# A hybrid decoder trunk with top-2 experts: order of the h links among the weight splits, and 64-row writes of the light experts' results

## Chip, cores and metric

The kernel runs on one core of one Trainium2 chip. The metric is the device time of one execution in microseconds (us). Two DeepNorm layers are computed for 256 tokens of width 1024; the second layer has eight experts.

## The reference, cut to what matters

```python
D_MODEL, SEQ, N_EXPERTS, TOP_K, D_FF_EXPERT = 1024, 256, 8, 2, 3584

def swiglu(x, wg, wu, wd):
    return (jax.nn.silu(x @ wg) * (x @ wu)) @ wd

def moe_swiglu(x, w_router, we_gate, we_up, we_down):
    logits = (x @ w_router).astype(jnp.float32)
    top_vals, top_idx = lax.top_k(logits, TOP_K)
    gates = jax.nn.softmax(top_vals, axis=-1)
    combine = jnp.einsum("bske,bsk->bse", jax.nn.one_hot(top_idx, N_EXPERTS), gates)
    out = jnp.zeros_like(x)
    for e in range(N_EXPERTS):
        out = out + combine[..., e:e + 1] * swiglu(x, we_gate[e], we_up[e], we_down[e])
    return out

for i in range(2):
    mix = hybrid_mixer(x, ...)                         # short convolution and spatial gating
    x = layer_norm(ALPHA * x + mix, ln1_g[i], ln1_b[i])
    ffn = swiglu(...) if i == 0 else moe_swiglu(...)   # layer 1: the experts
    x = layer_norm(ALPHA * x + ffn, ln2_g[i], ln2_b[i])
```

All tensors are float32. The change touches only the expert layer, which fills the span from about 380 us on.

## The kernel before, in words

**Pieces of weights.** All weights come from DRAM in pieces of 1 MB (128 partitions x 2048 float32), by DMAs that SyncE issues (`load`, L405) into a ring of six slots, `raw`. Each float32 product is made from rounded parts: ScalarE rounds a piece into `w_hi` (`split_hi`, L615, its copy is L620), VectorE subtracts it from the whole into `w_lo` (`split_lo`, L981, its subtraction is in the helper at L979), and TensorE multiplies with both. `w_hi` and `w_lo` have four slots each. So `split_hi(p)` waits for the landing of piece p and for TensorE's last use of piece p-4, `split_lo(p)` waits for `split_hi(p)`, and SyncE issues piece p+6 when `split_lo(p)` is done.

**Steps.** Each expert's inner width is cut into 7 steps of 512 columns, which makes 56 steps. A step takes six pieces: two of gate, two of up, two of down. With b = `step_at(i)`, pieces b and b+1 are the gate of step i, b+2 and b+3 its up, b+4 and b+5 the down of step i-1, and b+6 begins the gate of step i+1. The four experts with the most tokens are "heavy" (H, up to 128 tokens, three matmuls for each weight block), the four others "light" (L, up to 64 tokens, whose two rounded parts stand side by side, two matmuls for each block). `ORDER` (L75) fixes the order: four H, then L and H by turns with three extra H, then seven L.

**The engines' order in step i**, written out by hand. TensorE (L2173): gate of i; the turning of h of step i-1 (`turn_h`: four transposes, L1965, for H; sixteen folding matmuls, L1972, for L), which signals `e_hT`; the up of i; the down of i-1 (L1631 to L1633 for H, L2009 and L2010 for L), which waits for the low part of h (`e_hT_lo`) and for the two down pieces.

ScalarE (L872): where i-1 is light, the copy of its up sums (L809); split_hi of b+1 to b+4; `leave_gate(i)` (L803 or L805, reads the gate sums); then the links of h: for H `round_h(i-1)` (L813) after `e_hT`, for L `silu_few(i-1)` (L817) after `e_hT` and `round_few(i-1)` (L821) after VectorE's `times_few`; then split_hi of b+5 and b+6. VectorE (L1489): split_lo of b+1 to b+4; for H `rest_of_h` (L1354), for L `times_few` (L1358) and `rest_of_few` (L1362), all after ScalarE's links; split_lo of b+5 and b+6; where i is heavy, `times_up(i)` (L1350).

Both engines work in order: an instruction that waits holds all that stand behind it.

**Results.** When an expert is complete, ScalarE copies its sums to `ys_rows` (L841; for a light one 64 rows at L839, to which VectorE adds the other half of the sums, L1376) and GpSimd writes them to `slot_rows` in DRAM (L572), all 128 rows whatever the expert. Seven experts are written so: four heavy, three light (the last light one stays on the chip). After the last write GpSimd gathers for each token the rows of its two experts from `slot_rows` (L597), by row numbers that VectorE works out in `usable_choices` (L1406) in step 2, with 128 rows for each expert; VectorE adds them in steps 53 and 54 (L1466).

Of the kernel before, what the change touches and what calls it, by code (L numbers as in the profile page):

```python
# [4 lines left out]
P = 128  # L5
# [9 lines left out]
def hybrid_trunk_kernel(nc, x_in, w_in, conv_w, v_g, v_b, w_s, b_s, out_g, w_out, ln1_g, ln1_b, ln2_g, ln2_b,  # L15
# [62 lines left out]
    def light(i):  # L78
        return ORDER[i] == "L"
# [13 lines left out]
    def block_of(kind, k):  # L93
        return k if kind == "H" else HEAVIES + k
# [28 lines left out]
    with ctx:  # L123
# [56 lines left out]
        slot_rows = nc.dram_tensor("slot_rows", [(E - 1) * P, D], f32, kind="Internal").ap()  # L180
# [81 lines left out]
        combine_last = ranking[:, 304:304 + NT]  # L262
        usable_rows, usable_gates, usable_tmp = (ranking[:, a:a + NT * E].rearrange("p (n e) -> p n e", n=NT)
# [246 lines left out]
        def _(pool):  # L510
# [57 lines left out]
            def write_rows(j):  # L568
                kind, k = KEPT[j]
                r0 = block_of(kind, k) * P  # L570
                pool.wait_ge(ys_kept, j + 1)
                pool.dma_start(slot_rows[r0:r0 + P, :], ys_rows[:]).then_inc(ys_written, 16)  # L572
# [32 lines left out]
        def _(act):  # L605
# [16 lines left out]
            def splits(first, last):  # L622
                for p in range(first, last + 1):
                    split_hi(p)
# [247 lines left out]
            for i in range(N_STEPS):  # L872
                b = step_at(i)
                if i:
                    if light(i - 1):
                        leave_up(i - 1)
                    splits(b + 1, b + 2)
                    if kept_at(i) is not None:
                        keep_ys(kept_at(i))
                    splits(b + 3, b + 4)  # L880
                leave_gate(i)
                if i == 0:
                    split_hi(b + 4)
                elif light(i - 1):
                    silu_few(i - 1)
                    round_few(i - 1)
                    splits(b + 5, b + 6)
                else:
                    round_h(i - 1)
                    splits(b + 5, b + 6)  # L890
                after_up(i)
# [76 lines left out]
        def _(dve):  # L968
# [410 lines left out]
            def over_tokens(a):  # L1379
                return a.unsqueeze(1).to_broadcast([P, NT, E])  # L1380
# [25 lines left out]
            def usable_choices():  # L1406

                for a, first in ((is_light, 0.0), (block_at, 0.0), (not_last, 1.0)):
# [3 lines left out]
                step(nc.vector.tensor_scalar_add(block_at[:, 1:E], ranks, 1.0 - LIGHTS))  # L1412
# [4 lines left out]
                step(nc.vector.scalar_tensor_tensor(out=block_at, in0=is_light, scalar=float(HEAVIES + LIGHTS - 1),  # L1417
                                                    in1=block_at, op0=ALU.mult, op1=ALU.add))
                step(nc.vector.scalar_tensor_tensor(out=wide_count, in0=slot_iota[:, 0:E], scalar=-1.0 / 16,
# [5 lines left out]
                step(nc.vector.scalar_tensor_tensor(out=usable_rows, in0=over_tokens(block_at), scalar=float(P),  # L1425
# [63 lines left out]
            for i in range(N_STEPS):  # L1489
                b = step_at(i)  # L1490
                if i:
                    splits(b + 1 if i > 1 else b + 2, b + 3)
                    if kept_at(i) is not None and KEPT[kept_at(i)][0] == "L":
                        fold_ys(kept_at(i))
                    split_lo(b + 4)
                if i == 0:
                    splits(b + 4, b + 5)
                elif light(i - 1):
                    times_few(i - 1)
                    rest_of_few(i - 1)  # L1500
                    splits(b + 5, b + 6)
                else:
                    rest_of_h(i - 1)
                    splits(b + 5, b + 6)
                if not light(i):
                    times_up(i)
                after_up(i)
# [737 lines left out]
```

## Time and profile before

| | us |
|---|---|
| median of 3 runs (1306.07 to 1307.63) | 1307.62 |
| the profiled execution, its own time | 1306.71 |
| its span, first to last instruction | 1305.0 |
| TensorE busy | 1242.2 (95%) |
| VectorE busy | 1105.3 (85%) |
| ScalarE busy | 930.3 (71%) |
| GpSimd busy | 49.5 (4%) |

The span is 1.7 us shorter than the execution's own time, and that is 0.9 us below the median. The mean granted TensorE clock is 0.994 of full speed. The DMA engines moved 435 MB; in the 40 equal slices of the span their mean busy share is nine tenths or more from the thirteenth slice to the thirty-ninth. A busy share is an average: which engine sets the time of a stretch is read from the waits and the timeline. Where a matmul row shows 0.39 us, the next one starts 0.23 us later, since matmuls are pipelined.

### The profile page before, as it was taken

To read this page: it belongs to the slowest core of one execution; us is meant where nothing else is said; L and a number is where in the kernel's file an instruction comes from. 1 tells how busy PE (TensorE), PEld (TensorE's weight loads), DVE (VectorE), ACT (ScalarE), POOL (GpSimd) and SP (SyncE) were. 2 spreads that over 40 slices of the span, in tenths; PEclk is the share of its full clock that TensorE was granted. 3 is DMA by queue.
4 is the path that set the end of the run, shared out by engine and by line. 5 is a ranking of instruction groups with operands and counts; after the bars stand their busy time and mean duration, and the time that the engine had idled before them with its cause. 6 is when DMAs were issued, how large, how long until landed. Compare 5 with 4: busy or idle time off the path is not lost.

```text
span 1305.0 us, 15584 instructions
## 1 busy us (share of the span) xinstructions
PE 1242.2 (95%) x6145; PEld 1026.3 (79%) x6145; DVE 1105.3 (85%) x872; ACT 930.3 (71%) x747; POOL 49.5 (4%) x57
## 2 busy tenths in 40 slices
PE   9999999999999999999999999999999999998875
PEld 8988888888887877878777777777788777777654
DVE  6987555577989999989898989988989998898886
ACT  5575444464877887877777878777778877786773
POOL 0100000001012000000000000000000000000010
PEclk9999999999999999999999999999999999999999
DMA  9948555546569999999999999999999999999991
GB/s 321 344 143 272 187 189 191 193 140 215 190 221 347 398 397 390 398 399 398 397 389 400 397 401 397 397 389 397 396 395 400 397 396 398 397 396 403 397 397 69
DMA packets 190082, 435.25 MB, mean 334 GB/s; under 512 B 8196, under 2 KB 50228, under 8 KB 175668
## 3 DMA queue, kind: packets, MB, share of 16 engines
q1 hardware_dynamic: 186272, 421.06, 86.7%
q0 software_dynamic: 3648, 13.11, 3.0%
q8 instruction: 50, 0.82, 0.3%
q14 instruction: 28, 0.23, 0.0%
q10 hardware_dynamic: 84, 0.02, 0.0%
HBM read 428.40 MB, written 5.77 MB: 333 GB/s over the span
## 4 chain that ended last, share of the span: by engine, by line
PE 41%; DVE 32%; DMA 18%; ACT 7%; issue 2%; SPq 0%; DVEq 0%; ACTq 0%
DVE w_lo L979 28%; DMA raw<-in_we_down 17%; ACT w_hi L620 7%; PE turn L1743 4%; PE turn L1740 4%; PE accp L1631 4%; PE accp L1632 4%; PE accp L1633 4%; PE turn L1631 3%; PE turn L1633 3%; PE turn L1632 3%; PE turn L1742 2%; PE turn L1741 2%; DVE y_work L1350 1%; PE turn L1972 1%
## 5 line engine op out<-in xcount | busy, mean ns | idle before, releaser
L979 DVE TENSOR_TENSOR w_lo<-raw,w_hi 128x2048 fp32r<-128x2048 f32 (+1 forms) x401 | 895.6, 2266 | 112.9 <-ACT w_hi L620 110.9
L620 ACT CAST w_hi<-raw 128x2048 fp32r<-128x2048 f32 x395 | 749.7, 1912 | 161.6 <-DMA raw<-in_we_up 59.5
L1998 PE MATMUL turn<-w_hi,t_both 128*128 128x512 f32 x448 | 185.2, 413 | 16.2 <-DVE w_lo L979 13.1
L1999 PE MATMUL turn<-w_lo,t_both 128*128 128x512 f32 x448 | 177.4, 396 | 0.0
L1631 PE MATMUL turn<-w_hi,a_hi 128*128 128x512 f32 x440 | 174.3, 396 | 1.8 <-DVE w_lo L979 1.2
L1633 PE MATMUL turn<-w_hi,a_lo 128*128 128x512 f32 x440 | 171.6, 390 | 0.0
L1632 PE MATMUL turn<-w_lo,a_hi 128*128 128x512 f32 x440 | 171.4, 390 | 0.0
L1998 PEld LDWEIGHTS turn<-w_hi,t_both 128*128 128x128 f32 x448 | 85.3, 191 | 53.7 <-DVE w_lo L979 34.5
L1631 PE MATMUL accp<-w_hi,hT_hi 128*128 128x512 f32 x224 | 90.5, 404 | 16.3 <-DVE hT_lo L979 16.3
L1631 PEld LDWEIGHTS turn<-w_hi,a_hi 128*128 128x128 f32 x440 | 82.7, 188 | 19.5 <-DVE w_lo L979 1.8
L1999 PEld LDWEIGHTS turn<-w_lo,t_both 128*128 128x128 f32 x448 | 85.4, 191 | 15.9
L1633 PEld LDWEIGHTS turn<-w_hi,a_lo 128*128 128x128 f32 x440 | 82.6, 188 | 17.6
L1632 PEld LDWEIGHTS turn<-w_lo,a_hi 128*128 128x128 f32 x440 | 82.7, 188 | 16.3
L2009 PE MATMUL accp<-w_hi,hT_hi 128*128 128x512 f32 x216 | 85.8, 397 | 10.2 <-DVE w_lo L979 7.9
L1740 PE MATMUL turn<-t_both,w_hi 128*128 128x512 f32 x232 | 91.8, 396 | 0.0
L1743 PE MATMUL turn<-t_both,w_hi 128*128 128x512 f32 x232 | 91.8, 396 | 0.0
L1632 PE MATMUL accp<-w_lo,hT_hi 128*128 128x512 f32 x224 | 88.1, 393 | 0.0
L1633 PE MATMUL accp<-w_hi,hT_lo 128*128 128x512 f32 x224 | 87.8, 392 | 0.0
L2010 PE MATMUL accp<-w_lo,hT_hi 128*128 128x512 f32 x216 | 84.3, 390 | 0.0
L1631 PEld LDWEIGHTS accp<-w_hi,hT_hi 128*128 128x128 f32 x224 | 42.3, 189 | 33.9 <-DVE hT_lo L979 25.6
L1742 PE MATMUL turn<-t_both,w_lo 128*128 128x256 f32 x232 | 64.6, 278 | 0.0
L1741 PE MATMUL turn<-t_both,w_lo 128*128 128x256 f32 x232 | 64.3, 277 | 0.0
(291 smaller groups left out, 1591.7 us busy)
## 6 DMA issues: line engine op xcount, KB each, us to landing
raw<-in_we_gate SPq DMA_DIRECT2D x112, 1024.0 KB, 10.2
raw<-in_we_up SPq DMA_DIRECT2D x112, 1024.0 KB, 11.3
raw<-in_we_down SPq DMA_DIRECT2D x112, 1024.0 KB, 10.6
raw<-in_w_in SPq DMA_DIRECT2D x18, 1024.0 KB, 9.0
raw<-in_w_down SPq DMA_DIRECT2D x11, 1024.0 KB, 5.0
raw<-in_w_gate SPq DMA_DIRECT2D x10, 1024.0 KB, 5.2
raw<-in_w_up SPq DMA_DIRECT2D x10, 1024.0 KB, 5.2
raw<-in_w_out SPq DMA_DIRECT2D x8, 1024.0 KB, 10.3
```

Of the source, the lines that this page charges most:

```text
L620: nc.scalar.copy(w_hi[:, p % PARTS, :], raw[:, p % RING, :]).then_inc(hi_done, 1)
L979: return nc.vector.tensor_tensor(out, whole, hi.bitcast(f32), ALU.subtract)
L1631: nc.tensor.matmul(to, lh, rh, start=start, stop=False, **group)
L1632: nc.tensor.matmul(to, lh, rl, start=False, stop=False, **group)
L1633: return nc.tensor.matmul(to, ll, rh, start=False, stop=stop, **group)
L1740: nc.tensor.matmul(whole, wh[:, k, at], xT_pair[:, k, :], start=(k == 0), stop=False)
L1741: nc.tensor.matmul(first, wl[:, k, at], xT_hi[:, k, :], start=False, stop=False)
L1742: nc.tensor.matmul(first, wl[:, k + 1, at], xT_hi[:, k + 1, :], start=False, stop=False)
L1743: last = nc.tensor.matmul(whole, wh[:, k + 1, at], xT_pair[:, k + 1, :], start=False, stop=(k == KD - 2))
L1998: nc.tensor.matmul(to, few[:, k, :], wh[:, kk, :], start=(k == 0), stop=False)
L1999: last = nc.tensor.matmul(to, few[:, k, :], wl[:, kk, :], start=False, stop=(k == KD - 1))
L2009: nc.tensor.matmul(accp[:, 2 + c, :], left, wh[:, j, cols], start=(first and j == 0), stop=False)
```

## The change

The rows of the light results lie in `slot_rows` behind those of the heavy ones, 64 for each (`first_row` takes the place of `block_of`); GpSimd writes 64 rows for a light expert; `usable_choices` works out the first row in units of 64, with two more small instructions. On ScalarE in each step from 1 on, the first link of h stands behind split_hi of b+3, that is ahead of split_hi of b+4 and of `leave_gate(i)`; a light h's second link, `round_few`, stands behind split_hi of b+4. `leave_gate(i)` follows. On VectorE the first link (`times_few`, or `rest_of_h` for a heavy h) stands ahead of split_lo of b+4 and a light h's `rest_of_few` behind it. The order of TensorE and of SyncE is not changed, and neither are the ring of six slots and the four slots of `w_hi` and `w_lo`.

```diff
--- before.py
+++ after.py
@@ -90,8 +90,8 @@
     def rank(kind, k):
         return k if kind == "L" else LIGHTS + k - 1
 
-    def block_of(kind, k):
-        return k if kind == "H" else HEAVIES + k
+    def first_row(kind, k):
+        return k * P if kind == "H" else HEAVIES * P + k * FEW
 
     LAST_ONE = ("L", LIGHTS - 1)
     FETCHED = (("L", 0), ("H", 1), ("L", 1), ("H", 2), ("L", 2), ("H", 3), LAST_ONE)
@@ -177,7 +177,7 @@
         ys_rows = sb("ys_rows", [P, D])
         more_rows = sb("more_rows", [P, D])
 
-        slot_rows = nc.dram_tensor("slot_rows", [(E - 1) * P, D], f32, kind="Internal").ap()
+        slot_rows = nc.dram_tensor("slot_rows", [HEAVIES * P + (LIGHTS - 1) * FEW, D], f32, kind="Internal").ap()
         token_rows = nc.dram_tensor("token_rows", [TOK, D], f32, kind="Internal").ap()
 
         v = work[:, 0:1024].rearrange("p (n c) -> p n c", n=NT)
@@ -260,6 +260,7 @@
         wide_slot = ranking[:, 280:280 + NT * E].rearrange("p (n e) -> p n e", n=NT)
         wide_count = ranking[:, 296:296 + E]
         combine_last = ranking[:, 304:304 + NT]
+        light_less = ranking[:, 306:306 + E]
         usable_rows, usable_gates, usable_tmp = (ranking[:, a:a + NT * E].rearrange("p (n e) -> p n e", n=NT)
                                                  for a in (320, 336, 352))
 
@@ -567,9 +568,10 @@
 
             def write_rows(j):
                 kind, k = KEPT[j]
-                r0 = block_of(kind, k) * P
+                r0 = first_row(kind, k)
                 pool.wait_ge(ys_kept, j + 1)
-                pool.dma_start(slot_rows[r0:r0 + P, :], ys_rows[:]).then_inc(ys_written, 16)
+                count = FEW if kind == "L" else P
+                pool.dma_start(slot_rows[r0:r0 + count, :], ys_rows[0:count, :]).then_inc(ys_written, 16)
 
             def fetch_tokens(f):
                 pool.wait_ge(tokens_known, f // 2 + 1)
@@ -877,17 +879,19 @@
                     splits(b + 1, b + 2)
                     if kept_at(i) is not None:
                         keep_ys(kept_at(i))
-                    splits(b + 3, b + 4)
+                    split_hi(b + 3)
+                    if light(i - 1):
+                        silu_few(i - 1)
+                        split_hi(b + 4)
+                        round_few(i - 1)
+                    else:
+                        round_h(i - 1)
+                        split_hi(b + 4)
                 leave_gate(i)
-                if i == 0:
-                    split_hi(b + 4)
-                elif light(i - 1):
-                    silu_few(i - 1)
-                    round_few(i - 1)
+                if i:
                     splits(b + 5, b + 6)
                 else:
-                    round_h(i - 1)
-                    splits(b + 5, b + 6)
+                    split_hi(b + 4)
                 after_up(i)
             leave_up(N_STEPS - 1)
             split_hi(MOE_AT + MOE_PIECES - 1)
@@ -1409,20 +1413,25 @@
                     nc.vector.memset(a[:, 0:1], first)
                 nc.vector.tensor_scalar(is_light[:, 1:E], ranks, LIGHTS - 0.5, None, ALU.is_lt)
                 nc.vector.tensor_scalar(not_last[:, 1:E], ranks, float(rank(*LAST_ONE)), None, ALU.not_equal)
-                step(nc.vector.tensor_scalar_add(block_at[:, 1:E], ranks, 1.0 - LIGHTS))
+                step(nc.vector.tensor_scalar(block_at[:, 1:E], ranks, float(P // FEW), (1.0 - LIGHTS) * (P // FEW),
+                                             ALU.mult, ALU.add))
+                step(nc.vector.scalar_tensor_tensor(out=light_less, in0=is_light, scalar=FEW / P - 1.0, in1=block_at,
+                                                    op0=ALU.mult, op1=ALU.mult))
                 nc.vector.scalar_tensor_tensor(out=wide_slot, in0=over_tokens(is_light), scalar=float(FEW),
                                                in1=slot_of[:, :, 0:E], op0=ALU.mult, op1=ALU.add)
                 nc.vector.scalar_tensor_tensor(out=wide_count, in0=is_light, scalar=float(FEW), in1=key,
                                                op0=ALU.mult, op1=ALU.add)
-                step(nc.vector.scalar_tensor_tensor(out=block_at, in0=is_light, scalar=float(HEAVIES + LIGHTS - 1),
+                step(nc.vector.scalar_tensor_tensor(out=block_at, in0=is_light,
+                                                    scalar=float(HEAVIES * P // FEW + LIGHTS - 1),
                                                     in1=block_at, op0=ALU.mult, op1=ALU.add))
+                step(nc.vector.tensor_tensor(block_at, block_at, light_less, ALU.add))
                 step(nc.vector.scalar_tensor_tensor(out=wide_count, in0=slot_iota[:, 0:E], scalar=-1.0 / 16,
                                                     in1=wide_count, op0=ALU.mult, op1=ALU.add))
                 step(nc.vector.tensor_reduce(most, wide_count, X, ALU.max))
                 nc.vector.tensor_copy(most_i, most[0:1, :])
                 nc.vector.scalar_tensor_tensor(out=usable_tmp, in0=wide_slot, scalar=P - 0.5, in1=over_tokens(not_last),
                                                op0=ALU.is_lt, op1=ALU.mult)
-                step(nc.vector.scalar_tensor_tensor(out=usable_rows, in0=over_tokens(block_at), scalar=float(P),
+                step(nc.vector.scalar_tensor_tensor(out=usable_rows, in0=over_tokens(block_at), scalar=float(FEW),
                                                     in1=slot_of[:, :, 0:E], op0=ALU.mult, op1=ALU.add))
                 nc.vector.tensor_tensor(usable_rows, usable_rows, usable_tmp, ALU.mult)
                 nc.vector.tensor_tensor(usable_gates, combine, usable_tmp, ALU.mult)
@@ -1492,16 +1501,16 @@
                     splits(b + 1 if i > 1 else b + 2, b + 3)
                     if kept_at(i) is not None and KEPT[kept_at(i)][0] == "L":
                         fold_ys(kept_at(i))
-                    split_lo(b + 4)
                 if i == 0:
                     splits(b + 4, b + 5)
                 elif light(i - 1):
                     times_few(i - 1)
+                    split_lo(b + 4)
                     rest_of_few(i - 1)
                     splits(b + 5, b + 6)
                 else:
                     rest_of_h(i - 1)
-                    splits(b + 5, b + 6)
+                    splits(b + 4, b + 6)
                 if not light(i):
                     times_up(i)
                 after_up(i)
```

## Rows read from the trace of the kernel before

**Rows 1.** Busy time by stretches: the engines, granted clock, DMA share, GB/s.

```profile
core 0: us, PE busy (x) PEld busy (x) DVE busy (x) ACT busy (x) POOL busy (x), PEclk, DMA share, GB/s
457.84:1183.14 725.30, 698.25 (x3221) 564.41 (x3220) 658.10 (x381) 576.25 (x419) 10.52 (x12) 1.00 1.04 397
1183.14:1272.01 88.87, 72.86 (x321) 55.23 (x320) 75.64 (x45) 66.25 (x52) 5.72 (x4) 0.96 1.04 398
```

**Rows 2.** Waits between 560 and 1250 us: total us, times, longest.

```profile
DVE w_lo L979 <- ACT w_hi L620: 60.1, 97, 2.8
...
ACT w_hi L620 <- DMA raw<-in_we_up: 52.9, 67, 3.4
...
ACT w_hi L620 <- DMA raw<-in_we_down: 23.3, 42, 0.7
```

**Rows 3.** Timeline of ScalarE: start, us, engine, line, operation, idle before.

```profile
1055.26 1.91 ACT L620 CAST w_hi<-raw 128x2048 fp32r<-128x2048 f32 x1 [0.56 <-DMA raw<-in_we_down]
...
1058.16 0.39 ACT L817 ACTIVATE few_work<-turn 128x256 f32<-128x256 f32 x1 [0.51 <-PE turn L1972]
1059.86 0.41 ACT L821 CAST hT_hi<-few_work 128x256 fp32r<-128x256 f32 x1 [1.31 <-DVE few_work L1358]
1060.17 5.53 ACT L620 CAST w_hi<-raw 128x2048 fp32r<-128x2048 f32 x3
...
1071.06 1.91 ACT L620 CAST w_hi<-raw 128x2048 fp32r<-128x2048 f32 x1 [0.52 <-DMA raw<-in_we_down]
...
1073.35 0.59 ACT L813 CAST hT_hi<-turn 128x512 fp32r<-128x512 f32 x1
1073.83 1.92 ACT L620 CAST w_hi<-raw 128x2048 fp32r<-128x2048 f32 x1
```

**Rows 4.** Timeline of VectorE in the same stretch.

```profile
1062.11 4.50 DVE L979 TENSOR_TENSOR w_lo<-raw,w_hi 128x2048 fp32r<-128x2048 f32 x2 [1.39 <-ACT w_hi L620]
1066.52 0.68 DVE L1350 TENSOR_TENSOR y_work<-turn,y_work 128x512 f32<-128x512 f32 x1
1067.12 8.89 DVE L979 TENSOR_TENSOR w_lo<-raw,w_hi 128x2048 fp32r<-128x2048 f32 x4
```

**Rows 5.** Timeline of TensorE in the same stretch, at the joints of its work.

```profile
1056.14 1.98 PE L1972 MATMUL turn<-fold,y_work 128*128 128x64 f32 x16
...
1067.12 0.39 PE L1998 MATMUL turn<-w_hi,t_both 128*128 128x512 f32 x1
...
1069.46 0.50 PE L1998 MATMUL turn<-w_hi,t_both 128*128 128x512 f32 x1 [0.37 <-DVE w_lo L979]
...
1071.42 0.63 PE L1965 MATMUL turn<-ident,y_work 128*128 128x128 f32 x4
...
1076.67 0.50 PE L1631 MATMUL accp<-w_hi,hT_hi 128*128 128x512 f32 x1 [0.67 <-DVE hT_lo L979]
...
1082.24 0.39 PE L1631 MATMUL turn<-w_hi,a_hi 128*128 128x512 f32 x1
...
1087.69 1.98 PE L1972 MATMUL turn<-fold,y_work 128*128 128x64 f32 x16
```

**Rows 6.** Timeline of VectorE near the end.

```profile
1260.80 4.49 DVE L979 TENSOR_TENSOR w_lo<-raw,w_hi 128x2048 fp32r<-128x2048 f32 x2 [1.39 <-ACT w_hi L620]
1265.21 1.28 DVE L1466 SCALAR_TENSOR_TENSOR x<-ys_rows,small,x 128x1024 f32<-128x1024 f32 x1
```

**Rows 7.** Timeline of TensorE near the end.

```profile
1251.62 0.79 PE L1998 MATMUL turn<-w_hi,t_both 128*128 128x512 f32 x1 [2.61 <-DVE w_lo L979]
...
1254.91 1.98 PE L1972 MATMUL turn<-fold,y_work 128*128 128x64 f32 x16
```

**Rows 8.** Instructions on slot_rows (min, median, max ns) and their landing.

```profile
L572 POOL DMA_DIRECT2D slot_rows<-ys_rows x7: 533/562/589, 550.1 to 1182.1; - x7
...
DMA to landing us min/median/max: 6.3/7.1/9.0
```

## The prediction

> **What bounds the kernel now.** I read the busy times by stretches first. The stretches are cut where TensorE starts folding a light h: in step 5, in step 50 and in step 55. In the first one, 725.3 us long, the DMA engines are busy throughout at 397 GB/s, while TensorE is busy 698 us, VectorE 658 and ScalarE 576 [rows 1]. TensorE's 96% contain short stalls, so I read the waits next: ScalarE's roundings wait for landings (52.9 and 23.3 us for up and down pieces), VectorE's subtractions for ScalarE (60.1 us) [rows 2]. So the weight stream sets the time of the expert steps. The compute engines are close behind it, and the question is how close. For that I follow one pair of steps in the timelines: step 42 (heavy, with a light h to turn) and step 43 (light, with a heavy h), 1058 to 1090 us.
>
> In step 42 the fold ends at 1056.14 + 1.98 = 1058.12 [rows 5]. The rounding of b+4 had started at 1055.26 [rows 3], 2.9 us **before** that. In step 43 the heavy h's transposes end at 1071.42 + 0.63 = 1072.05 [rows 5], and the rounding of b+4 had started at 1071.06 [rows 3], 1.0 us before. In both the link of h is not ready when ScalarE comes to b+4. The change puts the link ahead of b+4, on an engine that works in order: the rounding of b+4 will wait for TensorE. The reader should see that these waits are new, and that everything behind b+4 moves too.
>
> **The pair with the new order.** Zero is the end of the fold (1058.12). Steps between starts, from the rows: a link of a light h 0.31 (1059.86 to 1060.17), a rounding 1.85 (5.53 for three), a 512-column copy 0.48 (1073.35 to 1073.83) [rows 3]; a subtraction 2.2, its last one ending 2.29 after its start, and it starts 1.94 after its rounding (1060.17 to 1062.11); times_up 0.60 [rows 3, 4].
>
> Step 42: silu_few 0.04; rounding of b+4 0.35; round_few 2.2; leave_gate 2.5; rounding of b+5 3.0; its subtraction 4.95. Today this one starts at 1062.11, which is 3.99 [rows 4]: **1.0 us later**. It carries on: b+6 7.15, times_up 9.35, subtraction of the next b+1 from 9.95 to 12.25. TensorE waits for that piece for the second half of the light gate; today it starts it at 1069.46 (11.34), having waited 0.37 [rows 5]. From there to the turn 1.96, the transposes 0.63: the heavy h is turned at 12.3 + 1.96 + 0.63 = 14.9, today 13.93.
>
> Step 43: round_h 14.95, rounding of b+4 15.4, its subtraction 17.4 to 19.7. The heavy down needs it; today TensorE starts that down at 1076.67 (18.55), after a wait of 0.67 for h's low part [rows 5]. So 19.7, **1.1 us later**; the earlier h gains nothing, since the piece itself is now the late one. (b+5: leave_gate 17.3, rounding 17.8, subtraction 19.7 to 22.0, in time for the second half.) From there down 5.57 (1076.67 to 1082.24), gate 5.45, fold 1.98 [rows 5]: 32.7. The compute loop would need **32.7 us for a pair**. The same pair takes 31.55 now (1056.14 to 1087.69) [rows 5].
>
> **The stretch.** Between the folds of steps 5 and 50 lie 21 pairs and 3 extra heavy steps; an extra heavy step is up, down and gate, 5.57 + 5.57 + 5.45 and 0.4 for the transposes, 17.0 us [rows 5]. New: 21 x 32.7 + 3 x 17.0 = 737.7 us against 725.3 [rows 1], **+12.4**. As the compute loop then exceeds the stream, DMA no longer decides there. The slack of the ring hides none of it, because the lateness is TensorE's own.
>
> **Folds of results and gathered tokens on VectorE** are some 1.2 and 0.7 us each, mostly beside the new waits: +1, between 0 and 8. **Steps 1 to 4**, all heavy with the same new wait: TensorE has 17 us of work a step and the link's wait fits beside its 5.57 us of up: +1, between 0 and 2.5. **Two more small instructions in usable_choices**: 0.4 us once, in step 2, while TensorE has work: 0.
>
> **The light steps at the end.** From the start of the subtraction of b+1: 2.29 to its end, 1.96 gate half, 1.98 fold, 4.95 to the subtraction of b+5, two of 2.2: 15.6 us a step, and 2.6 more in two of them (add_rows, 1.28 each [rows 6]). Five steps: 83.2 us. Where the granted clock falls, a light gate half takes 1254.91 - 1251.62 = 3.3 us in place of 1.96 [rows 7]; I allow two of these, 85.8. Now this stretch takes 88.87 [rows 1], because the stream is full there too; with the ring filled ahead by the late engines it is not waited for. **-3**, between -5.5 and +1. What follows the last step is the same work: 0.
>
> **The light writes.** The queue lands 512 KB in 6.3 to 9.0 us [rows 8], beside the weights. Three writes lose 0.26 MB each: 0.79 MB at 397 GB/s [rows 1] is 2.0 us if the stream sets the time, and 0 in my sum, where it doesn't; the bounds are these two.
>
> That queue row can't show whether a 64-row write is any shorter. The Trainium skill has a rule that speaks against it: in "SBUF — State Buffer", section "Door 1: The DMA port swizzle", partitions 0 to 63 reach only 8 of the 16 ports, so 64 rows would take as long as 128 rows. By it the 2.0 us would be 0 whatever bounds the kernel; no row here shows it.
>
> **Sum.** 12.4 + 1 + 1 - 3 = +11.4 us on the profiled execution's 1306.7: 1318.1. The median of the runs shown lies 0.9 above that execution: **1319**.
>
> **Rivals.** What a measurement can tell from no change is 0.2%, 2.6 us.
>
> (1) My forecast, the compute loop takes over: 1319, with its bounds 1311 to 1330. Chance 0.64.
>
> (2) The other side: the stream goes on setting the time. The place is the pair, the price 2.0 us for the writes and about 1 in the light steps. It decides if the pair's loop stays under what the stream needs; 725.3 less three extra heavy steps is 674.3 for 21 pairs, 32.1 us each [rows 1, 5]. So 0.6 us too much in my pair would do it. For it: the stream is at its limit in the whole stretch [rows 1], and TensorE's stall at the heavy down would go if b+4 were ready. Against: both links come after the start of b+4 in the pair read. 1307.6 - 3 = 1304.5. Chance 0.18, about two thirds of it past 0.2%.
>
> (3) The lateness is partly given back (heavy traffic hides it in some pairs, the end returns the rest): 1307 to 1311. Chance 0.10.
>
> (4) TensorE's new stalls, some 1 us twice a pair, make its granted clock fall more often. Today that is rare: 1.00 in the long stretch, 0.96 in the light steps with their longer waits [rows 1, 7]. Each fall costs 1.3 us at a gate half. In each pair that would be 21 x 1.3 = 27 us more, 1346; in a third of them 1328. Chance 0.08, at 1328 to 1346.
>
> The Trainium skill's page "TensorE: Matmul & The Clock Gate" says in Part 1 that the gate halves the clock of a TensorE that has been idle and gives it back to a busy one; by that the change could only lower it, and the trace agrees in that its dip lies behind the 2.61 us wait.
>
> **Range and chances.** Below 1304 and above 1334 I leave about one in ten each: 1304 to 1334; the likeliest case alone has 1311 to 1330. Faster: two thirds of (2) and a little of (3), 0.14. Same: the rest of (2) and most of (3), 0.14. Slower 0.72.
>
> **What would show it.** In the changed trace: ScalarE's idle time before silu_few and the heavy round_h, released by TensorE's turn, 2 to 3 us each in a heavy step with a light h and about 1 to 2 after a heavy one, in nearly all of 46 steps; its waits for landings nearly gone; a fold-to-fold pair of about 32.7 us; DMA moving some 390 GB/s in the first stretch; the rounding of b+5 some 1 us later against the fold's end. TensorE's wait for h's low part should give way to a wait for w_lo. I am wrong if the landings are still waited for as now and pairs stay at 31.6 to 32.1: then (2). If the granted clock is below 0.97 in the long stretch, it is (4).

## The result, and the profile after

| | before | after |
|---|---|---|
| median of 4 runs, us | 1307.34 | 1325.91 (1325.13 to 1327.94) |
| ratio, 95% interval | | 1.0146 (1.0129 to 1.0164) |
| profiled execution's span | 1305.0 | 1324.8 |
| fold of step 5 begins | 457.84 | 460.99 |
| from there to the fold of step 50 | 725.30 | 743.62 |
| from there to the fold of step 55 | 88.87 | 85.97 |
| from there to the end of the span | 32.99 | 34.22 |

The kernel is 18.6 us (1.5%) slower; 1319 was forecast, with 1304 to 1334 around it. The lower four rows cut the span as the prediction did. The loss of 18.3 us in the long stretch is larger than all the rest; 3.15 us are lost before it, 2.9 come back behind it.

The page of the changed kernel (TensorE's busy time, and the GB/s in 40 slices):

```profile
span 1324.8 us, 15586 instructions
...
PE 1251.0 (94%) x6145; PEld 1028.2 (78%) x6145; DVE 1104.1 (83%) x874; ACT 913.6 (69%) x747; POOL 48.3 (4%) x57
...
GB/s 321 341 133 286 190 192 191 191 151 178 212 217 368 393 381 371 379 398 386 393 383 388 385 393 396 391 367 397 388 359 401 392 382 393 387 379 401 397 402 65
```

The same stretches as [rows 1], in the changed kernel:

```profile
core 0: us, PE busy (x) PEld busy (x) DVE busy (x) ACT busy (x) POOL busy (x), PEclk, DMA share, GB/s
460.99:1204.61 743.62, 703.40 (x3221) 564.53 (x3220) 656.64 (x382) 562.83 (x419) 9.16 (x12) 1.00 1.03 386
1204.61:1290.58 85.97, 72.05 (x321) 54.41 (x320) 75.78 (x45) 63.94 (x50) 8.44 (x4) 0.97 1.04 399
```

In the long stretch the DMA engines still show a busy share over 1, but they move 386 GB/s in place of 397 [rows 1]. So a busy share of that height doesn't say that the stream sets the time. The GB/s and the waits for landings tell it. TensorE's mean granted clock is 1.00 as before, so the clock isn't the cause of the loss. It does fall to half twice for a short time, and what that costs is worked out below, where the stretch is compared with the forecast.

The waits between 560 and 1270 us:

```profile
ACT few_work L819 <- PE turn L1981: 95.8, 22, 5.3
ACT hT_hi L815 <- PE turn L1974: 57.1, 21, 4.3
...
DVE few_work L1362 <- ACT few_work L819: 44.7, 19, 3.4
DVE w_lo L983 <- ACT w_hi L622: 36.6, 39, 1.4
...
PE accp L1640 <- DVE w_lo L983: 20.6, 18, 1.9
...
ACT w_hi L622 <- DMA raw<-in_we_up: 9.1, 12, 1.4
```

[rows 2] has waits of the roundings for landings: 52.9 us for up pieces. 9.1 are left. In their place stand ScalarE's waits for TensorE, 95.8 us for folds and 57.1 for transposes, and behind them VectorE's for ScalarE. By themselves they don't show a loss. TensorE waits 20.6 us (18 times) for the subtraction of a piece at the heavy down; before it waited there for h's low part (14.6 us, 17 times).

The pair of steps 42 and 43, with [rows 3 to 5] beside it. ScalarE:

```profile
1076.74 0.39 ACT L819 ACTIVATE few_work<-turn 128x256 f32<-128x256 f32 x1 [5.29 <-PE turn L1981]
1077.02 1.91 ACT L622 CAST w_hi<-raw 128x2048 fp32r<-128x2048 f32 x1
1078.82 0.41 ACT L823 CAST hT_hi<-few_work 128x256 fp32r<-128x256 f32 x1
1079.12 0.61 ACT L807 ACTIVATE y_work<-turn 128x512 f32<-128x512 f32 x1
1079.61 9.14 ACT L622 CAST w_hi<-raw 128x2048 fp32r<-128x2048 f32 x5
1091.54 0.59 ACT L815 CAST hT_hi<-turn 128x512 fp32r<-128x512 f32 x1 [2.79 <-PE turn L1974]
1092.02 1.91 ACT L622 CAST w_hi<-raw 128x2048 fp32r<-128x2048 f32 x1
```

VectorE:

```profile
1077.16 0.43 DVE L1362 TENSOR_TENSOR few_work<-turn,few_work 128x256 f32<-128x256 f32 x1 [2.48 <-ACT few_work L819]
1078.96 2.29 DVE L983 TENSOR_TENSOR w_lo<-raw,w_hi 128x2048 fp32r<-128x2048 f32 x1 [1.38 <-ACT w_hi L622]
1081.17 0.42 DVE L983 TENSOR_TENSOR hT_hi<-few_work,hT_hi 128x256 fp32r<-128x256 f32 x1
1081.56 4.49 DVE L983 TENSOR_TENSOR w_lo<-raw,w_hi 128x2048 fp32r<-128x2048 f32 x2
1085.97 0.68 DVE L1354 TENSOR_TENSOR y_work<-turn,y_work 128x512 f32<-128x512 f32 x1
1086.58 6.68 DVE L983 TENSOR_TENSOR w_lo<-raw,w_hi 128x2048 fp32r<-128x2048 f32 x3
1093.18 0.68 DVE L983 TENSOR_TENSOR hT_lo<-turn,hT_hi 128x512 fp32r<-128x512 f32 x1
1093.96 13.39 DVE L983 TENSOR_TENSOR w_lo<-raw,w_hi 128x2048 fp32r<-128x2048 f32 x6
```

TensorE, at the joints:

```profile
1074.72 1.98 PE L1981 MATMUL turn<-fold,y_work 128*128 128x64 f32 x16
...
1088.91 0.50 PE L2007 MATMUL turn<-w_hi,t_both 128*128 128x512 f32 x1 [0.68 <-DVE w_lo L983]
...
1090.87 0.63 PE L1974 MATMUL turn<-ident,y_work 128*128 128x128 f32 x4
...
1096.39 0.47 PE L1640 MATMUL accp<-w_hi,hT_hi 128*128 128x512 f32 x1 [0.96 <-DVE w_lo L983]
...
1107.41 1.87 PE L1981 MATMUL turn<-fold,y_work 128*128 128x64 f32 x15
```

The fold ends at 1074.72 + 1.98 = 1076.70, the zero of the forecast's schedule. ScalarE's silu (L819) comes 0.04 later after 5.29 us idle, the rounding of b+4 at 0.32, round_few 2.1, leave_gate 2.4, the rounding of b+5 at 2.9 and its subtraction (1081.56) at 4.86; 4.95 was forecast. TensorE's second half of the light gate begins at 12.2 (forecast 12.3), having waited 0.68; the transposes end at 14.8 (14.9); the heavy down waits 0.96 for the piece and begins at 19.7 (19.7). From fold to fold 1107.41 - 1074.72 = 32.69 us, where 32.7 was forecast.

### The profile page after: what moved, and what is told of

It reads as the page before. It is cut to its first block, busy times and chain, and to the rows that moved or that the text cites. A ratio compares the mean times of both kernels' runs of the same rounds, so it can differ in the third digit from the quotient of the medians.

```text
span 1324.8 us, 15586 instructions
## 1 busy us (share of the span) xinstructions
PE 1251.0 (94%) x6145; PEld 1028.2 (78%) x6145; DVE 1104.1 (83%) x874; ACT 913.6 (69%) x747; POOL 48.3 (4%) x57
## 4 chain that ended last, share of the span: by engine, by line
PE 62%; DVE 26%; ACT 7%; issue 3%; DMA 2%; SPq 0%; DVEq 0%; ACTq 0%
DVE w_lo L983 22%; ACT w_hi L622 7%; PE accp L1640 7%; PE accp L1642 6%; PE accp L1641 6%; PE turn L1640 5%; PE turn L1642 5%; PE turn L1641 5%; PE turn L1749 4%; PE turn L1752 4%; PE turn L1981 4%; PE turn L2007 3%; PE turn L2008 2%; PE turn L1751 2%; PE turn L1750 2%
## 5 line engine op out<-in xcount | busy, mean ns | idle before, releaser
L622 ACT CAST w_hi<-raw 128x2048 fp32r<-128x2048 f32 x395 | 741.5, 1917 | 55.9 <-PE accp L1642 29.3
L2007 PE MATMUL turn<-w_hi,t_both 128*128 128x512 f32 x448 | 187.3, 418 | 22.8 <-DVE w_lo L983 16.0
L819 ACT ACTIVATE few_work<-turn 128x256 f32<-128x256 f32 x28 | 10.8, 385 | 122.8 <-PE turn L1981 122.8
L815 ACT CAST hT_hi<-turn 128x512 fp32r<-128x512 f32 x28 | 16.4, 587 | 82.8 <-PE turn L1974 82.8
```

Of the source, the lines that this page charges most:

```text
L622: nc.scalar.copy(w_hi[:, p % PARTS, :], raw[:, p % RING, :]).then_inc(hi_done, 1)
L2007: nc.tensor.matmul(to, few[:, k, :], wh[:, kk, :], start=(k == 0), stop=False)
```

## The experiments

Each is compared with the kernel before in runs on the same chip, whose medians were 1307.1 to 1307.7 us; the differences below are to that median, unless another run is named.

### 64-row writes alone

The changed kernel with both loops over the steps as before. Its edit on ScalarE and on VectorE:

```diff
-                    split_hi(b + 3)
-                    if light(i - 1):
-                        silu_few(i - 1)
-                        split_hi(b + 4)
-                        round_few(i - 1)
-                    else:
-                        round_h(i - 1)
-                        split_hi(b + 4)
+                    splits(b + 3, b + 4)
                 leave_gate(i)
-                if i:
-                    splits(b + 5, b + 6)
-                else:
-                    split_hi(b + 4)
+                if i == 0:
+                    split_hi(b + 4)
+                elif light(i - 1):
+                    silu_few(i - 1)
+                    round_few(i - 1)
+                    splits(b + 5, b + 6)
+                else:
+                    round_h(i - 1)
+                    splits(b + 5, b + 6)
                 after_up(i)
...
+                    split_lo(b + 4)
                 if i == 0:
                     splits(b + 4, b + 5)
                 elif light(i - 1):
                     times_few(i - 1)
-                    split_lo(b + 4)
                     rest_of_few(i - 1)
                     splits(b + 5, b + 6)
                 else:
                     rest_of_h(i - 1)
-                    splits(b + 4, b + 6)
+                    splits(b + 5, b + 6)
```

> The 64-row writes and the new row numbers alone; the links of h stand as in the kernel before. Theory (the weight stream sets the time, the three writes lose 0.79 MB of it): 2.0 us less than before, 1305.3, with ScalarE's waits for landings unchanged. Rival (a 64-row write takes as long as a 128-row one, by the port rule of the Trainium skill's page SBUF - State Buffer): 0, 1307.3, and its landing time stays near the 7.1 us median. Second rival (the new row numbers or writes cost something): over 1309.

Measured 1305.90 us, ratio 0.9984 (0.9975 to 0.9993): 1.6 us less (0.9 to 3.3 by the interval), where the theory had 2.0. Pairs and waits are as before (52.3 us for landings of up pieces). The writes by size (number, KB each, median us from issue to landing), in the kernel before and then in this run:

```profile
slot_rows<-ys_rows POOLq DMA_DIRECT2D x7, 512.0 KB, 6.7
```

```profile
slot_rows<-ys_rows POOLq DMA_DIRECT2D x4, 512.0 KB, 6.7
...
slot_rows<-ys_rows POOLq DMA_DIRECT2D x3, 256.0 KB, 5.8
```

A write of 64 rows lands in 5.8 us where one of 128 rows takes 6.7. In the other runs with 64-row writes and whole weight pieces its median is 5.6 to 6.1, and 6.8 against 7.0 with the order on ScalarE alone. So it is shorter, but by far less than half. (The 7.1 us that the expectation takes from [rows 8] is a median over all transfers of `slot_rows`, the four gathers too.) By the port rule, which the Trainium skill states in "SBUF — State Buffer", section "Door 1: The DMA port swizzle", a 64-row write would take as long as a 128-row one; beside this stream it doesn't, and a gain of 0 lies outside the interval. The gain agrees with the bytes saved, within that interval.

### The order alone

The kernel before with both loops over the steps from the changed one, the same diff read backwards:

```diff
-                    splits(b + 3, b + 4)
+                    split_hi(b + 3)
+                    if light(i - 1):
+                        silu_few(i - 1)
+                        split_hi(b + 4)
+                        round_few(i - 1)
+                    else:
+                        round_h(i - 1)
+                        split_hi(b + 4)
                 leave_gate(i)
...
```

> The new order of the links alone, with 128-row writes. Theory (all of the loss is the order, and the stream no longer decides): the changed kernel's time to within 1 us, 1325 to 1327, with pairs of 32.7 us from fold to fold. Rival (the stream still decides in part): 2 us above the changed kernel, 1328.

Measured 1326.04 us, ratio 1.0136 (1.0121 to 1.0152), the changed kernel's time. The order carries the whole loss. Beside it the smaller writes bring nothing that these runs can tell: what they save counts in the kernel that waits for bytes.

### Only light, only heavy links in the new place

The changed kernel, in which a condition chooses between the two orders; for the heavy links it reads `i > 0 and not light(i - 1)`:

```diff
+    def SOON(i):
+        return i > 0 and light(i - 1)
...
                     split_hi(b + 3)
-                    if light(i - 1):
+                    if not SOON(i):
+                        split_hi(b + 4)
+                    elif light(i - 1):
                         silu_few(i - 1)
...
                 leave_gate(i)
+                if i and not SOON(i):
+                    if light(i - 1):
+                        silu_few(i - 1)
+                        round_few(i - 1)
+                    else:
+                        round_h(i - 1)
...
+                if i and not SOON(i):
+                    split_lo(b + 4)
...
                     times_few(i - 1)
-                    split_lo(b + 4)
+                    if SOON(i):
+                        split_lo(b + 4)
                     rest_of_few(i - 1)
...
-                    splits(b + 4, b + 6)
+                    splits(b + 5 if not SOON(i) else b + 4, b + 6)
```

> The changed kernel, but only a light h has its links in the new place; a heavy h has them as before. Theory (a compute loop of 31.2 us for a pair before, plus 1.0 us for the light link, against some 32.1 that the stream needs, so that one of the two delays is almost covered): 32.2 us for a pair in the compute loop, 21 x 0.1 = 2 us and 1 to 3 us where results are folded or tokens summed: 1308 to 1313. Rival (the two delays simply add, each costs half of the 18.5 us): 1316.

> The changed kernel, but only a heavy h has its link in the new place; a light h has them as before. Theory: the heavy down waits for the piece b+4 by 1.1 us more, less what TensorE waits for h's low part today (0.67), so 31.7 to 32.3 us for a pair in the compute loop, about the stream's: 1306 to 1312. Rival (the delays simply add, each costs half): 1316.

Light links alone: 1313.76 us, ratio 1.0047 (1.0034 to 1.0061). Heavy link alone: 1308.13, ratio 1.0004 (0.9995 to 1.0013). Against the writes alone (1305.9) that is +7.9 and +2.2, and both together +20.0: far from additive, as the theory of a covered loop says. The heavy link's 2.2 us lie in steps 1 to 4: its fold 5 begins at 461.18 us, that of the writes alone at 457.53, and from there to fold 50 the two take 724.64 and 724.18. In the long stretch the heavy link alone costs nothing. The sizes were off for the light links: their pairs take 32.42 us (40 to 42 and on to 46 to 48: 32.46, 32.42, 32.42, 32.45), not 32.2, and the run is 0.8 above my range.

### The stream taken away

```diff
                 dst = raw[:, p % RING, :].rearrange("p (k f) -> p k f", k=src.shape[1])
+                if p >= MOE_AT + 22:
+                    part = src.shape[1] // 2
+                    dst, src = dst[:, 0:part], src[:, 0:part]
                 sp.dma_start(dst, src).then_inc(slot_filled[p % RING], 16)
```

> The kernel before with the stream taken away as a bound: from step 4 on each weight DMA loads only the first half of its piece (half of the experts' weights is left out, the engines work on what the slot held). All engines keep their work. Theory (the compute loop of the kernel before needs 31.2 us for a pair and only the stream holds it at 32): the stretch from the fold of step 5 to that of step 50 takes 21 x 31.2 + 3 x 17.0 = 706 and some 6 us for folded results and tokens, 712 in place of 725.3, and the whole run 1286 to 1294. Rival (the engines set the time before as well): within 4 us of 1307.

> The changed kernel with the same half loads from step 4 on (half of the experts' weights is left out). Theory (in the changed kernel the compute loop decides everywhere, the stream nowhere): nothing changes, 1323 to 1327, pairs of 32.7 us. Rival (a slower answer of the memory under the later issues carries part of the loss): clearly faster, under 1318.

Half loads in the kernel before: 1281.58 us, ratio 0.9803 (0.9788 to 0.9818). Its stretch from fold 5 to fold 50, 705.39 us (columns as in [rows 1]):

```profile
457.41:1162.80 705.39, 689.63 (x3222) 568.31 (x3221) 654.10 (x382) 573.26 (x419) 9.24 (x12) 1.00 0.70 209
```

Half loads in the changed kernel: 1323.43, ratio 1.0128 (1.0112 to 1.0143), and 742.42 us in the same stretch. Time between the turns of h (folds) of the steps named, us:

| steps | before | after | half, before | half, after | light links | ScalarE alone |
|---|---|---|---|---|---|---|
| 40 to 42 | 30.91 | 32.67 | 30.76 | 32.66 | 32.46 | 36.01 |
| 42 to 44 | 31.55 | 32.69 | 30.74 | 32.66 | 32.42 | 36.22 |
| 44 to 46 | 32.43 | 32.70 | 30.73 | 32.67 | 32.42 | 36.02 |
| 46 to 48 | 32.13 | 32.70 | 30.73 | 32.66 | 32.45 | 36.23 |
| 5 to 50 | 725.30 | 743.62 | 705.39 | 742.42 | 733.67 | 814.49 |

This is the deciding measurement. Without the stream the compute loop of before needs 30.73 us for a pair, and the stream holds it at 31 to 32.4, unevenly. In the changed kernel taking half of the bytes away changes 32.7 to 32.66. The loop grew by 1.93 us a pair, and only the part above the stream's pace costs time. The whole run with half loads is 2.5 us under the changed kernel, and the intervals of their ratios overlap. The 1.2 us between 743.62 and 742.42 are all in the stretch from fold 7 to fold 9, which takes 34.05 us with half loads and 35.23 in the changed kernel, where TensorE's clock falls in it. So the rival (under 1318) fails. The first run is faster than its range (1286 to 1294), because the loop of before is 0.5 us shorter than my 31.2.

### New order on ScalarE alone, on VectorE alone

The first is the changed kernel with this edit on VectorE:

```diff
+                    split_lo(b + 4)
                 if i == 0:
                     splits(b + 4, b + 5)
                 elif light(i - 1):
                     times_few(i - 1)
-                    split_lo(b + 4)
                     rest_of_few(i - 1)
...
-                    splits(b + 4, b + 6)
+                    splits(b + 5, b + 6)
```

The second is the changed kernel with ScalarE's loop as in the experiment on the writes:

```diff
-                    split_hi(b + 3)
-                    if light(i - 1):
-                        silu_few(i - 1)
...
+                    splits(b + 3, b + 4)
                 leave_gate(i)
...
```

> The changed kernel with the new order on ScalarE alone; VectorE has its order of before (the subtraction of b+4 ahead of the links). It asks on which engine the loss arises. Theory (the loss is the rounding of b+4 that stands behind the link on ScalarE; VectorE's old order makes it worse, since times_few must now stand behind that late piece and round_few and the rounding of b+5 behind times_few): from the fold's end the subtraction of b+5 starts at about 7.7 us in place of 4.95, so 35.4 us for a pair of light and heavy, 1326 + 21 x 2.7 + 5 x 2.7 = about 1395, 1370 to 1400. Rival (VectorE's new order carries the loss): 1307 to 1315.

> The changed kernel with the new order on VectorE alone; ScalarE has its order of before, so the rounding of b+4 doesn't wait for TensorE. Theory (ScalarE carries the whole loss): no loss. The stream bounds all but the last step; there VectorE's subtraction of b+5 starts at 3.4 us after the fold in place of 5.2, so 1303.5 to 1306 (the writes alone gave 1305.9). Rival (VectorE's wait for silu ahead of b+4 costs by itself): 1309 to 1317.

ScalarE alone: 1411.42 us, ratio 1.0789 (1.0773 to 1.0804), 11 us above the range but on the theory's side by far. Its ScalarE:

```profile
1099.84 0.39 ACT L819 ACTIVATE few_work<-turn 128x256 f32<-128x256 f32 x1 [5.29 <-PE turn L1981]
1100.12 1.90 ACT L622 CAST w_hi<-raw 128x2048 fp32r<-128x2048 f32 x1
1104.72 0.41 ACT L823 CAST hT_hi<-few_work 128x256 fp32r<-128x256 f32 x1 [2.69 <-DVE few_work L1362]
1105.03 0.59 ACT L807 ACTIVATE y_work<-turn 128x512 f32<-128x512 f32 x1
1105.52 9.11 ACT L622 CAST w_hi<-raw 128x2048 fp32r<-128x2048 f32 x5
...
1135.85 0.39 ACT L819 ACTIVATE few_work<-turn 128x256 f32<-128x256 f32 x1 [5.29 <-PE turn L1981]
```

round_few (L823) now stands 2.69 us idle for times_few, which VectorE does only behind the late b+4, and the rounding of b+5 begins 1105.52 - 1099.84 = 5.7 us after silu; in the changed kernel it is 1079.61 - 1076.74 = 2.9. The pair takes 36.2 us (forecast 35.4).

VectorE alone: 1304.13 us, ratio 0.9972 (0.9960 to 0.9984), no loss. Waits between 560 and 1180 us in it:

```profile
ACT w_hi L622 <- DMA raw<-in_we_up: 46.7, 57, 1.9
...
DVE few_work L1360 <- ACT few_work L819: 30.3, 17, 3.0
PE accp L1638 <- DVE w_lo L981: 27.8, 18, 2.8
```

VectorE waits for silu here too (30.3 us), and TensorE for the piece at the heavy down (27.8 us, more than in the changed kernel). But ScalarE again waits for landings (46.7 us): the stream is the bound, so these waits cost nothing. **The loss is what now stands behind a link on ScalarE**, and VectorE's part of the change softens it. Two things stand there: the rounding of b+4 and `leave_gate`. From the start of silu to the rounding of b+5 it is 2.87 us in the changed kernel and 2.01 before: the rounding of b+4 fills the 1.31 us in which ScalarE used to wait for times_few and some 0.4 more, and `leave_gate` adds 0.49. No run puts `leave_gate` back alone, so how the cost divides between the two isn't shown. At the heavy down it is the piece b+4 that TensorE waits for.

### The new order from step 5 on

```diff
+    def SOON(i):
+        return i > 4
```

> The changed kernel with the links of h where they were in steps 1 to 4 and the new order from step 5 on. It asks where the 3.0 us come from that the changed kernel is late by at the fold of step 5 (1.0 was in the sum). Theory (in the first heavy steps VectorE's small work for the router stands behind a longer chain of subtractions, and TensorE waits for it): 3 us less than the changed kernel, 1322 to 1324. Rival (the compute loop takes the gain back later, as the stream would then be waited for): 1325 to 1326.

Measured 1322.50 us, ratio 1.0115 (1.0100 to 1.0129); its fold 5 begins at 457.58, as before, and the later stretch takes 744.09. The first four steps cost 3.1 us and nothing gives them back. The changed kernel's TensorE there:

```profile
425.24 0.51 PE L1640 MATMUL turn<-w_hi,a_hi 128*128 128x512 f32 x1 [1.00 <-DVE w_lo L983]
...
449.81 0.47 PE L1640 MATMUL accp<-w_hi,hT_hi 128*128 128x512 f32 x1 [1.00 <-DVE w_lo L983]
```

It waits 1.00 us for the first piece behind the row numbers of step 2, and 1.00 us at the heavy down of step 4, for the piece b+4 as in the pair above. Each makes the next matmul start some 1.2 us late; the rest of the 3.1 lies in shorter gaps. The first instruction of the row numbers on VectorE, before and in the changed kernel:

```profile
418.08 0.17 DVE L1410 TENSOR_SCALAR ranking<-ranking 128x7 f32<-128x7 f32 x1
```

```profile
420.39 0.16 DVE L1414 TENSOR_SCALAR ranking<-ranking 128x7 f32<-128x7 f32 x1
```

They begin 2.3 us later, since VectorE has stood idle in that step for 1.18 us until round_h and for 1.11 us until the rounding of b+4. The run with heavy links alone has the same 3 us (its fold 5 begins at 461.18), the one with light links alone has none.

### The new order in steps 51 to 55 alone

```diff
+    def SOON(i):
+        return i > 50
```

> The 64-row writes, and the new order of the links in steps 51 to 55 alone, where step and predecessor are light; all earlier steps as in the kernel before. It asks what the 3 us that the changed kernel got back between the folds of steps 50 and 55 are due to. Theory (the ring had been filled ahead, the order gives at most 0.3 us a step): 0 to 1 us less than the writes alone, 1304.5 to 1306.5. Rival (the order itself helps light steps): 1302 to 1303.

Measured 1305.61 us, ratio 0.9986 (0.9977 to 0.9995): the writes alone gave 1305.90, so the order brings nothing that these runs can tell. The 2.9 us that the changed kernel gets back between folds 50 and 55 come from the ring being further ahead when the stretch begins: the stream runs at full rate in it in both kernels, and 88.87 us at 398 GB/s are 35.4 MB, 85.97 us at 399 GB/s are 34.3 MB, about one piece less (2.6 us). With the stream halved, that stretch takes 85.3 us in the order of before and 83.5 in the new one, so the order would be worth 1.9 us where no stream covers it.

### Versions meant to beat both

The kernel of the experiment on the writes, with this edit on ScalarE:

```diff
                 elif light(i - 1):
                     silu_few(i - 1)
-                    round_few(i - 1)
-                    splits(b + 5, b + 6)
+                    split_hi(b + 5)
+                    round_few(i - 1)
+                    split_hi(b + 6)
```

> A version meant to beat both: the 64-row writes, the links where the kernel before has them, and for a light h the rounding of b+5 between silu_few and round_few (where ScalarE waits for times_few today) in place of behind both. Theory: in the steps with the stream as bound nothing; in the five light steps at the end the subtraction of b+5 starts about 1.4 us sooner after the fold, of which the stream lets some 2 to 4 us through in all: 1301.5 to 1304. Rival (the stream covers it there too): 1305.5 to 1306.5, as with the writes alone. Second rival (round_few and so the low part of h comes later and TensorE waits for it): over 1307.

Measured 1303.07 us, ratio 0.9968 (0.9955 to 0.9980): 4.1 us under the kernel before and 22.8 under the changed one. VectorE in step 55, this version first, then the writes alone:

```profile
1273.37 0.42 DVE L1361 TENSOR_TENSOR few_work<-turn,few_work 128x256 f32<-128x256 f32 x1
1274.96 0.43 DVE L982 TENSOR_TENSOR hT_hi<-few_work,hT_hi 128x256 fp32r<-128x256 f32 x1 [1.17 <-ACT hT_hi L823]
1275.30 6.69 DVE L982 TENSOR_TENSOR w_lo<-raw,w_hi 128x2048 fp32r<-128x2048 f32 x3
```

```profile
1274.43 0.42 DVE L1360 TENSOR_TENSOR few_work<-turn,few_work 128x256 f32<-128x256 f32 x1
1275.32 0.43 DVE L981 TENSOR_TENSOR hT_hi<-few_work,hT_hi 128x256 fp32r<-128x256 f32 x1 [0.47 <-ACT hT_hi L823]
1277.13 6.69 DVE L981 TENSOR_TENSOR w_lo<-raw,w_hi 128x2048 fp32r<-128x2048 f32 x3 [1.39 <-ACT w_hi L622]
```

From times_few to the subtraction of b+5 it is 1.93 us in place of 2.70, and the fold of step 55 to the next turn takes 7.37 us in place of 9.50. But between folds 50 and 55 it takes 89.59, no less than 88.22, with a lower mean clock of TensorE (0.92 against 0.98), and from fold 5 to fold 55 the two take 812.7 and 812.4. So my size was right and my place was not: the stream is the bound up to the last step, and only there the shorter chain counts.

The second has the same ScalarE loop and keeps VectorE's new order, as the experiment with VectorE alone did:

```diff
                     silu_few(i - 1)
-                    round_few(i - 1)
-                    splits(b + 5, b + 6)
+                    split_hi(b + 5)
+                    round_few(i - 1)
+                    split_hi(b + 6)
```

> The new order on VectorE, the old one on ScalarE but with the rounding of b+5 between silu_few and round_few: both versions that should gain in the last step, together, with the 64-row writes. Theory (the subtraction of b+5 is then held by VectorE's own work at 3.4 us after the fold, so the second edit adds nothing to the first): 1302.5 to 1304.5, as the better of the two alone. Rival (the gains add): 1300 to 1302.

Measured 1303.62 us, ratio 0.9972 (0.9964 to 0.9981). The gains don't add; the three versions of 1303.1 to 1304.1 can't be told apart.

## Why the prediction was right

**The bound and its distance.** Right: the stream was the bound before, with the engines close behind. The loop of before is 30.73 us, shown by the halved stream; the prediction gave no row for it and the experiments' 31.2 was an estimate that was 0.5 too long. The 31.55 us that it set its 32.7 against is a pair paced by the stream.

**The pair.** Right to 0.1 us at each joint, 32.69 measured for 32.7. The reason given holds too: with light links alone the pair is 32.42, with both 32.7, with ScalarE's order as before no loss. The two delays of 1.0 and 1.1 us don't share the growth evenly, though: of the loop's 1.93 us the light link alone makes 1.69.

**The stretch.** 737.7 was the sum for pairs and heavy steps, 743.62 measured. Pairs without other work took 32.66 to 32.75 us and the three with an extra heavy step 49.70, 49.70 and 48.62. The missing 6 us are in the **term for folded results and tokens, mis-sized at +1**: 7 to 9 takes 35.23, 18 to 20 34.20, 33 to 35 35.20 us; three more pairs are 0.3 to 0.6 long, and two stretches are about 1 short. Two things make the long ones. The first is TensorE's wait: 1.82 us for the tokens' part (0.35 before), and 1.9 us at the down behind a folded result. The latter was 1.8 us before as well (1.82 and 1.81), where the stream's pace covered it. The second is **TensorE's clock**, to which this term gave nothing. TensorE in step 8 and in step 34, and the granted clock (the third number from the end) right behind the first wait:

```profile
507.10 0.50 PE L2007 MATMUL turn<-w_hi,t_both 128*128 128x512 f32 x1 [1.82 <-DVE a_lo L983]
...
947.60 0.47 PE L1640 MATMUL accp<-w_hi,hT_hi 128*128 128x512 f32 x1 [1.88 <-DVE w_lo L983]
```

```profile
507.90:511.20 3.30, 3.30 (x9) 2.63 (x8) 3.30 (x2) 0.34 (x1) 0.00 (x0) 0.50 0.99 364
```

The clock falls from 2.4 to 1.2 GHz for a few matmuls, which then start 0.43 us apart in place of 0.23. The same pairs without a fall, in other runs of this order, take 34.05 (half loads) and 33.61 (the order from step 5 on): so a fall costs 1.2 to 1.6 us, and the two make 2.8 of the 6. The kernel before has one such fall in its stretch, behind a wait of 1.81 us at 933.57. Whether a wait of that length is followed by a fall differs from run to run (18 to 20 has a wait of 1.91 us and none). The bound of 8 had allowed for the sum.

**Steps 1 to 4**, put at +1 with an upper bound of 2.5, cost 3.15. That is outside my bound. I looked at TensorE's 17 us a step alone. VectorE's chain is what counts there too: TensorE waits once for the piece behind the row numbers of step 2, to which I gave no cost, and once for the piece at the heavy down of step 4.

**The light steps.** 85.8 forecast, 85.97 measured, -2.9 for the -3. The ring ahead is borne out as the reason, not the order. But that the stream "is not waited for" is wrong: it runs at 399 GB/s and ScalarE waits 7.2 us for up pieces there, so the agreement to 0.2 us is in part luck. Behind them I had 0; it is +1.2, and that is the clock again. From fold 55 to the next turn the changed kernel takes 10.65 us, and 9.51 before; behind a wait of 2.60 us the clock is halved while it folds (3.51 us in place of 1.98):

```profile
1290.58 3.51 PE L1981 MATMUL turn<-fold,y_work 128*128 128x64 f32 x16
```

The order alone also has 10.65 with a fall there; the order from step 5 on, whose clock is back early in the fold, has 9.53.

**The writes.** 0 in the sum, as the order alone shows; 1.6 us where the stream is the bound. The row was misread: 6.3 to 9.0 us in [rows 8] are all transfers of `slot_rows`, and 9.0 is a gather; the seven writes have a median of 6.7.

Sum: 12.4 + 6 + 3.1 - 2.9 + 1.2 = 19.8 us in the profiled executions, against 11.4 forecast. So the mechanism and the pair were right, and the range held because its upper side had room for terms that were put too small. Rivals: (2) the stream goes on setting the time falls with the halved stream, and so does (3). (4) falls as the main cause, with a mean clock of 1.00 and two falls in 24 pairs and extra steps, but its mechanism is there in small. Signs misjudged in size: ScalarE's wait before silu was put at 2 to 3 us and is 5.29 in the pair and 4.4 on average, that before the heavy round_h at 1 to 2 and is 2.7 (95.8 us in 22 waits, 57.1 in 21); its waits for landings, 52.9 us before, are nearly gone, and it arrives early.

## What to carry to other kernels

On an engine that works in order, a piece of the stream that stands behind a link whose input comes from the engine that the stream feeds waits with it. Here it was cheaper to put the link behind the pieces that were ready before it. Before moving work, measure how far the compute loop lies under the stream (halve the bytes and look at the period): here it was about 1 us a pair (725.3 against 705.4 us over the stretch), and two moves that cost 2.2 and 7.9 us alone cost 20 together. Look also for waits that the stream's pace covers today, such as the 1.8 us behind a folded result: they count once the loop is the bound, and TensorE's clock can fall behind them.

## What the runs showed that was not expected

The DMA engines' busy share stays at 1.03 while they move 386 GB/s in place of 397 in the long stretch, and with half of each piece it is 0.70 at 209 GB/s: the share falls less than the bytes. In the changed kernel TensorE's clock fell to half behind waits of 1.8 to 2.6 us, though not behind each of them. With the order on ScalarE alone, where VectorE waits 116 us for roundings, the granted clock is 0.974 over the span, against 0.991 in the changed kernel and 0.994 before; so part of that run's loss is TensorE's clock, which its expectation left out.
